# Attention outputs with features on the partitions, and probabilities scaled ahead of their transpose, in a six-layer transformer kernel

## The reference, cut to what matters

```python
for i in range(4):                       # first block: kinds A, B, C, A
    h = (mixer_a, mixer_b, mixer_c)[i % 3](x, ...)
    x = layer_norm(ALPHA * x + h, ...)
    x = layer_norm(ALPHA * x + swiglu(x, ...), ...)
# second block, twice: four branches (convolution, sparse attention over the
# 64 best keys, a gated recurrence, attention over 256 memory rows), gated,
# projected and added; then a gated feed-forward
```

## Time and profile before

| | |
|---|---|
| median of 3 runs | 2409.44 us (2409.36 to 2410.32) |
| span of the profiled execution | 2408.6 us |
| PE busy | 2375.2 us (99%) |
| PEld busy | 2001.8 us (83%) |
| DVE busy | 1633.0 us (68%) |
| ACT busy | 1122.9 us (47%) |
| POOL busy | 184.1 us (8%) |
| PE's share of the chain that ended last | 92% |

### The profile page before, as it was taken

The page is one execution under the profiler, slowest core; times in us unless marked ns, Lnnn a source line. Parts: engine busy times, 40 slices in busy tenths (PEclk is TensorE's granted clock), DMA queues, the critical chain, the costliest instruction groups (busy, mean ns, idle before and its releaser), DMA issues.

```text
span 2408.6 us, 33578 instructions
## 1 busy us (share of the span) xinstructions
PE 2375.2 (99%) x13648; PEld 2001.8 (83%) x13648; DVE 1633.0 (68%) x2282; ACT 1122.9 (47%) x1570; POOL 184.1 (8%) x190
## 2 busy tenths in 40 slices
PE   7999999999999999999999999999999999999999
PEld 5788888787888878887888888888888888988887
DVE  7866755557667576668776777677676577687664
ACT  4544344444443434435443455564444365574442
POOL 1210002021000320001100100000000000001000
PEclk9999999999999999999999999999999999999999
DMA  6465343335553446543755344444755344445652
GB/s 247 142 202 209 140 175 140 141 140 171 197 209 140 163 165 215 191 158 128 262 188 179 136 175 157 155 179 149 279 180 188 113 167 156 173 175 181 225 177 91
DMA packets 259080, 419.09 MB, mean 174 GB/s; under 512 B 11984, under 2 KB 149200, under 8 KB 258928
## 3 DMA queue, kind: packets, MB, share of 16 engines
q1 hardware_dynamic: 254064, 400.15, 46.7%
q0 software_dynamic: 4864, 16.80, 2.1%
HBM read 415.86 MB, written 1.05 MB: 173 GB/s over the span
## 4 chain that ended last, share of the span: by engine, by line
PE 92%; DVE 4%; ACT 2%; DMA 1%; issue 1%; POOL 0%; SPq 0%; DVEq 0%; ACTq 0%
PE bank_L L2431 21%; PE bank_L L2447 17%; PE bank_S L2811 8%; PE bank_T L2776 7%; PE bank_L L2776 7%; PE bank_O L2811 7%; PE bank_L L2428 4%; PE bank_T L2781 4%; PE bank_L L2781 4%; PE bank_O L2724 1%; DVE wlo L1631 1%; PE bank_S L2431 1%; PE bank_O L2431 1%; PE bank_T L2398 1%; PE bank_T L2707 1%; PE bank_T L2386 1%
## 5 line engine op out<-in xcount | busy, mean ns | idle before, releaser
L1631 DVE TENSOR_TENSOR wlo<-raw,whi 128x2048 fp32r<-128x2048 f32 x316 | 718.0, 2290 | 123.4 <-ACT whi L1237 123.0
L1237 ACT ACTIVATE whi<-raw 128x2048 fp32r<-128x2048 f32 x290 | 542.5, 1894 | 55.3 <-DMA raw<-in_w_out 13.2
L2431 PE MATMUL bank_L<-whi,xt 128*128 128x512 f32 (+2 forms) x1632 | 495.8, 386 | 3.3 <-ACT tok L1283 2.1
L2447 PE MATMUL bank_L<-whi,xt 128*128 128x512 f32 x1248 | 389.2, 393 | 3.3 <-DVE xt L1645 2.1
L2431 PEld LDWEIGHTS bank_L<-whi,xt 128*128 128x128 f32 x1632 | 295.9, 188 | 61.2 <-ACT tok L1283 3.3
L2431 PE MATMUL bank_L<-wlo,xt 128*128 128x512 f32 (+2 forms) x816 | 311.4, 382 | 0.0
L2447 PEld LDWEIGHTS bank_L<-whi,xt 128*128 128x128 f32 x1248 | 230.6, 188 | 51.9 <-DVE arena L1737 2.9
L1503 ACT ACTIVATE tok<-tok 128x256 f32<-128x256 f32 x96 | 40.1, 417 | 449.5 <-DVE tok L2137 449.5
L2447 PE MATMUL bank_L<-wlo,xt 128*128 128x512 f32 x624 | 243.6, 390 | 0.0
L2776 PE MATMUL bank_T<-xt,whi 128*128 128x512 f32 x768 | 192.3, 392 | 0.0
L2776 PE MATMUL bank_L<-xt,whi 128*128 128x512 f32 x768 | 191.7, 392 | 0.0
(11 more groups left out here) (353 smaller groups left out, 3630.3 us busy)
## 6 DMA issues: line engine op xcount, KB each, us to landing
raw<-in_w_gate_up SPq DMA_DIRECT2D x176, 512.0 KB, 5.9
raw<-in_w_in SPq DMA_DIRECT2D x72, 1024.0 KB, 6.8
draw<-in_w_down SPq DMA_DIRECT2D x44, 1024.0 KB, 6.2
raw<-in_ffn_w_up SPq DMA_DIRECT2D x88, 512.0 KB, 5.8
raw<-in_b_w_qkv SPq DMA_DIRECT2D x36, 1024.0 KB, 6.9
draw<-in_ffn_w_down SPq DMA_DIRECT2D x22, 1024.0 KB, 6.2
raw<-in_w_lift SPq DMA_DIRECT2D x16, 1024.0 KB, 6.2
raw<-in_a_w_qkv SPq DMA_DIRECT2D x12, 1024.0 KB, 8.2
```

The lines of the kernel that those rows point to most:

```text
L1237: act.activation(wide(whi, w, nkc, ncols)[:, ks, :], wide(raw, w, nkc, ncols)[:, ks, :], ACT.Copy) \
L1631: dve.tensor_tensor(wide(wlo, w, nkc, ncols)[:, ks, :], wide(raw, w, nkc, ncols)[:, ks, :], wide(whi, w, nkc, ncols)[:, ks, :].bitcast(F32 ...
L2431: mm = pe.matmul(banks[name][:, 0:st["ncols"]], xx[:, kk, t * P:(t + 1) * P], ww[:, kk, :], start=(kk == 0 and q == 0), stop=(kk == nkc - ...
L2447: mm = pe.matmul(banks[bank][:, :], xx[:, k, t * P:(t + 1) * P], ww[:, k, :], start=(k == 0 and q == 0), stop=(k == KC - 1 and q == 2))
```

## The change

It does the following things at once.

1. The product with values is turned round: the values (128 keys by 64 features) are the weights, and the transposed probabilities are streamed, 128 or 256 columns at a time. The even head of a pair writes partitions 0 to 63 of bank_O and the odd one 64 to 127. The output is there with features on the partitions, as the projection reads it. One bank holds four heads over 256 queries, and is held until it is split.
2. The transposes of the output (`turn_group` for these attentions, L2491), the evacuation to `r` or `arena`, and the later `halves`/`split` stages are gone. ACT copies bank_O into the high part (`group_high`), DVE subtracts for the low part (`group_low`), once for each bank. In B and C half of it goes to `yt_hi`, `yt_lo`, and half to `xt_hi`, `xt_lo`.
3. A query's sum is no longer on the partitions at the end, so the probabilities are scaled before their transpose. PE now waits for `scaled` where it waited for `p_done`.
4. In A and the sparse attention a new stage kind, `spread`, takes the place of `attention`. POOL scales (two instructions for a head, of 128 and 256 columns). The transpose comes three steps after the scores in A (two before), and still two in the sparse attention, where the products with values come up to one step later and for two heads at once. `sm` is a ring of five heads in A and of four in the sparse one, `pts` a ring of four.
5. In B and C ACT scales, in the same step as the exponentials. DVE takes the reciprocals of step i in step i (before: those of step i-1), ahead of `group_low`, rotations and `wlo` subtractions.
6. The rotations' scratch moves from `hg_values` to `r`.

The core of the diff:

```diff
 # POOL, kind "spread"
+                        pool.wait_ge(rl_done, k + 1)
+                        for row, (c0, c1) in enumerate(((0, P), (P, 3 * P))):
+                            q = slice(u["ps"] + c0, u["ps"] + c1)
+                            ins = pool.tensor_scalar(smflat[:, q], smflat[:, q], rl[:, k % 4, row:row + 1], None, ALU.mult)
+                        ins.then_inc(scaled, 1)
 # ACT, kind "paired"
-                    def pair_evacuate(j):
+                    def pair_scales(j):
                         act.wait_ge(rl_done, U0 + j + 1)
-                        act.wait_ge(pv_done, U0 + j + 1)
...
+                                ins = act.activation(smflat[:, q], smflat[:, q], ACT.Copy, scale=rl2[:, c:c + 1])
+                            ins.then_inc(scaled, 1)
+                    def group_high(g):
+                        to = st["to"]
+                        act.wait_ge(pv_done, V0 + (g + 1) * to["per"])
...
                         if 1 <= i <= len(J):
                             pair_copies(i - 1)
-                        if i >= 2:
-                            pair_evacuate(i - 2)
+                        if i < len(J):
+                            pair_scales(i)
+                        if i >= 2 and (i - 1) % st["to"]["per"] == 0:
+                            group_high((i - 2) // st["to"]["per"])
 # DVE, kind "paired"
+                    def group_low(g):
+                        to = st["to"]
+                        hi, lo = to["dst"][g]
+                        dve.wait_ge(thi_done, to["sg"] + g + 1)
+                        dve.tensor_tensor(lo, banks[st["ob"][g % 2]][:, :].rearrange("p (k s) -> p k s", s=SEQ), hi.bitcast(F32),
+                                          ALU.subtract).then_inc(tlo_done, 1)
...
                             pair_copies(i - 1)
-                            pair_reciprocal(i - 1)
+                        if i < len(J):
+                            pair_reciprocal(i)
+                        if i >= 2 and (i - 1) % st["to"]["per"] == 0:
+                            group_low((i - 2) // st["to"]["per"])
                         if i in st["ropes"]:
                             rotated(st["ropes"][i])
 # PE, kind "paired"
-                            pe.wait_ge(p_done, u["p0"] + 1)
+                            pe.wait_ge(scaled, u["sc0"] + 1)
...
+                        for two in zip(*(u["pv"] for u in J[j])):
+                            for w, (c, width, v, o1, first, last) in enumerate(two):
+                                c += J[j][w]["pts"]
+                                mm = pe.matmul(banks[name][w * HD:(w + 1) * HD, o0 + o1:o0 + o1 + width], v, pflat[:, c:c + width],
+                                               start=first, stop=last)
 # PE and DVE, kind "spread"
+                        pe.wait_ge(scaled, at["sc"] + i + 1)
...
+                    for i in range(st["steps"]):
+                        if i < len(U):
+                            maxima(i)
+                        if 1 <= i <= len(U):
+                            reciprocal(i - 1)
+                        if i > lag + 1 and (i - lag - 1) % 4 == 0:
+                            group_low((i - lag - 1) // 4 - 1)
+                        if 0 <= i - lag < len(U):
+                            copies(i - lag)
+                        if i in st["lows"]:
+                            split_lo(*st["lows"][i])
+                    group_low(len(U) // 4 - 1)
```

More of the change, by code:

```diff
@@ L498, in paired, with spread @@
                     n["tp"] += T
-                for g, when in at_groups.get(j, ()):
-                    turned["at_tp"][g], turned["when"][g] = n["tp"], (o_done, st["at"]["unit"] + when)
-                    n["tp"] += 1
             n["unit"] += len(pairs)
-            if turned:
-                for g in range(4):
-                    if turned["at_tp"][g] is None:
-                        turned["at_tp"][g], turned["when"][g] = n["tp"], (o_done, n["unit"])
-                        n["tp"] += 1
-            return st
+            n["pv"] += len(pairs)
+            return st
+        def spread(units, ready, first, behind, to, lag, ring, stride, lead=2, fill=(), lows=None, highs=None):
+            add("spread", units=units, ready=ready, first=first, behind=behind, to=to, lag=lag, lead=lead, fill=fill,
+                qb=SB if fill else QB, lows=lows or {}, highs=highs or {}, steps=len(units) + lag + 1)
+            for st in behind:
+                st["deferred"] = True
+            for st in fill:
+                st["kind"] = "fill"
+            for i, u in enumerate(units):
+                edge, ps = 1 if u["sink"] else 0, stride * (i % ring)
+                u["ps"], u["pts"] = ps + edge, 3 * P * (i % 4)
+                u["ends"] = ps
+                u["exp"] = [slice(ps, ps + edge + P), slice(ps + edge + P, ps + 3 * P + 2 * edge)]
+            n["seg"] += len(units)
+            n["ttr"] += T * len(units)
+            for q in ("p", "sc", "tp", "pt", "unit"):
+                n[q] += len(units)
+            n["pv"] += len(units) // 2
+            return (pv_done, n["pv"])
         def ffn(lhs, w_up, w_dn, alpha, evacuate=False, mem=None):
@@ L651, in build @@
                         dst = vv[g] if which == 2 else next_tok()
-                        after = [(o_done, n["unit"])] if which == 2 and n["unit"] else []
+                        after = [(pv_done, n["pv"])] if which == 2 and n["unit"] else []
                         if (which, g) == (2, 2):
@@ L1464, in _ @@
                             copies(i - 2)
-                        if st["rows"] and i == steps - 1:
-                            group_hi(st["rows"], 0)
-                            group_hi(st["rows"], 1)
                         if i >= 3:
@@ L2110, in _ @@
                             split_lo(*st["splits"][i])
-                        for g, _ in st["groups"].get(i, ()):
-                            group_lo(st["rows"], g)
                 elif st["kind"] == "ffn":
```

311 lines of the change are left out of this document (201 added, 110 removed).

## The result

The changed kernel takes 2439.31 us (median of 4 runs, 2435.62 to 2443.13) where the kernel before took 2409.4. The ratio is 1.0127, 95% interval 1.0113 to 1.0142: about 30 us slower. The prediction was 2409.7 with a range of 2400 to 2420, so the sign and the size are both missed. The span of the profiled execution is 2440.7 us, 32.1 more than before. It is the slowest of the four: its mean granted clock is 0.992, that of the other three 0.994.

A forecast was written before the change was run, and what follows sets the result against it. PE was taken to bound the kernel (busy 2375.2 of 2408.6 us), with DVE becoming A's bound. A -2.0, sparse -3.8, B +3.85 and C +2.2 sum to +.25, so 2409.7 us, range 2400 to 2420.

The forecast's parts named there:

- POOL's price: A: POOL's two scalings of a head take .95 us, between about .75 and 1.1, hidden under DVE's 1.27.
- DVE becomes the bound and the loop stays as long as it was: A: DVE needs 2.84 us per two heads, PE's old time; only the end gains, -1.0 a layer.
- The value products: Value blocks of two heads: .80 for 1.00 in A; in B 1.55 to 1.4, counted as -.7.
- halves of the array don't pair up: Rival: even and odd heads' streams into partition halves cost more than the narrow form; 2439 us, chance .04.
- the last rival: The change doesn't do what it says: removed instructions are covered by as many others; 2409 us, chance .04.
- three waits for bank_L: B: ACT's scalings delay bank_L's evacuation in three steps, by +.75, +1.0 and +1.25, together +3.0 us.
- dear scaling: Rival: ACT's scaling costs what the exponential does, .94, adding +4.5 in B and C; 2414.2 us, chance .12.
- The rotation at the end of the half: B, end of first half: bank copy and subtraction come before the rotation, so PE's transpose is +2.45 us later.
- +2.55 at the rotation: C, step 3: reciprocal, scalings, bank copy and subtraction now precede the rotation, making PE's transposes 2.55 us later.
- the sparse attention in sign and place: Two sparse layers: PE is gap-free, so removed work counts; -1.9 us each, after +.35 for head 0's wait.
- the cover that was missing: B and C: queues leave no slack at late places; the rival, that cover holds (2402 halfway), had chance .25.
- The rival of POOL and DVE blocking each other: A: DVE's two-column copies wait about .3 us for POOL's instructions, +9.6 over 32 heads; 2419.3 us, chance .13.

The follow-up runs named there:

- e1: Changed kernel with POOL's two scalings of a head in A cut to 8 columns each, result not normalised there: 2436.77 us, 29.0 over before.
- e12: Changed kernel with A's transposes four steps behind the scores instead of three: 2436.07 us, 29.2 over the kernel before.
- e9: Changed kernel with A's PE transposes moved ahead of the scores and DVE's copies ahead of the maxima: 2445.82 us, 38.4 over before.
- e13: Changed kernel with A's transposes four steps behind scores and another ACT and DVE order in B and C: 2416.54 us, 9.6 over before.
- e8: Kernel before the change, with the multiplications of C's step 3 rotation done five times: 2416.94 us, 9.1 over before.
- e3: Changed kernel with all work kept but another order on ACT and DVE in B and C: 2417.56 us, 9.8 over the kernel before.
- e7: Kernel before the change, with the multiplications of C's step 3 rotation done twice: 2411.22 us, 3.4 over before.

## Why the prediction was wrong

**POOL's price (A).** The step "for 128 and 256 columns: about .75 by the first, about 1.1 by the second" had both ends too low. The slope of 2 ns a column came from 8 and 16 columns, where 16 ns lie between two durations that are almost all start; the measured one is (927 - 607) / 128 = 2.5 ns, and the start .29, not .18. With 1.53 for a head POOL is above DVE's 1.27, and the sentence "so either is hidden but for the last head" fails: PE waited 4.3 us for scaled heads in the first A. But the price is not what A lost, since with the scalings cut to 8 columns (e1) as much was lost in other waits.

**"DVE becomes the bound and the loop stays as long as it was" (A).** This step failed: no wait of PE in the loop stood in the sum, and PE waited 7.0 us, for scaled heads and for copies. It compared rates. My account is that the loop is a chain: a head's way from scores to transposable probabilities (scores .86, maxima .86, exponentials .9, reciprocal behind the next maxima, POOL 1.53) against three steps, and values that wait for a copy behind the maxima. This is argued, not shown. e1 fits it (the waits stay with POOL's work taken away), but one step more (e12) gave some 0.8 us for both A together, of a rest of 5.3, and e9 made it worse. What is shown is that neither POOL's work nor ACT's help sets the time, and, by e13's trace, that with four steps DVE is the slowest engine, slowed by POOL. I had looked at each engine's sum and at the end of the loop, not at the way through it.

**The value products.** These were right. -.2 for two heads was taken in A, -.7 in B. From the start of a block to the start of the next, the four products of two heads cost .80 in A and in the sparse attention where 1.00 stood, as forecast. In B's first half:

```profile
439.80 1.53 PE L2742 MATMUL bank_O<-pts,arena 128*64 128x128 f32 x24
441.26 0.87 PE L2721 MATMUL bank_T<-ident,sm 128*128 128x128 f32 x6
```

1.46 against 1.55 before, and the narrow blocks .81 against .85: about half of the gain that was hoped for (1.4 and .75). This also settles the rival "halves of the array don't pair up". Its number, 2439, is the measured one by luck: its mechanism did not happen. Nor did that of the last rival: PE has 880 instructions fewer and ACT 96 (DVE has 2282 in both, where the prediction had its count fall).

**B.** PE at the places that the sum spoke of, and at the one that it didn't:

```profile
430.80 0.73 PE L2546 MATMUL bank_L<-whi,xt 128*128 128x512 f32 x2 [1.73 <-ACT tok L1323]
...
457.72 1.54 PE L2513 MATMUL bank_T<-ident,tok 128*128 128x128 f32 x6 [2.75 <-DVE tok L1820]
...
552.57 0.58 PE L2546 MATMUL bank_L<-whi,xt 128*128 128x256 f32 x2 [2.01 <-ACT arena L1323]
...
568.40 0.88 PE L2742 MATMUL bank_O<-pts,arena 128*64 128x128 f32 x12 [3.43 <-DVE xt L2201]
```

The three waits for bank_L were forecast at +.75, +1.0, +1.25 and are +1.04, +1.24, +1.54 (1.73, 1.93, 2.01 against .69, .69, .47): the mechanism was right, and the gap is the scaling's .93 in place of .75, the rival with "dear scaling". (That rival's own sum doesn't come out: six waits with two blocks each at .2 and C's four at .1 are 2.8, not 4.5.) The rotation at the end of the half was forecast at +2.45 and waits 2.75 against .32: +2.43. Missing from the sum were the waits for bank_O (3.43 and 1.2, the first for DVE's subtraction): a bank that holds four steps of one half is refilled only when it is split, and the split stands behind two scalings of .93. It was written in the change's description and not followed to PE.

**C.** +2.55 at the rotation, measured +3.87 (4.88 less 1.01). The queue is 2.9 of it: ACT was done with the exponentials at 861.94 - .24 = 861.70, and the rotation started at 864.56, the scalings being 1.50 where 1.1 was taken. The other part is POOL: its conversions now run beside two instructions of the rotation instead of one. In the kernel before, one already took 1.12 beside a conversion, where .28 is the time alone, which also means that 0.8 of the wait of 1.01 in the earlier trace rows was POOL's and not the queue's:

```profile
842.97 1.12 DVE L1753 TENSOR_TENSOR tok<-hg_values 128x128 f32<-128x128 f32 x1
```

**The clock.** No term at all. Each wait was costed once. By the windows PE ran at half the clock behind the long ones, and e8 measures 2.8 us for one such place. Of the 32 us, 17.5 are at the clock's account in the traced execution and the rest are the waits less the work removed. No rival has the clock either.

**Right:** the sparse attention in sign and place (-1.3 each instead of -1.9; PE waits 1.21 for head 0 where .35 was given, .58 of which is POOL's price), the value products, the places of the waits in B and C, and what moves them: the cover that was missing at the earlier trace rows was there once e3 had changed the queues. The rival of POOL and DVE blocking each other is real but small in the changed kernel: the copies of two columns have a mean of .195 where it was .150, 1.4 us for all 32. With POOL never idle (e13) the mean is .238, and in the loop's middle most take .36, as shown above (behind the count: shortest, median and longest ns):

```profile
L2082 DVE COPY sm<-sk x32: 148/192/380, 55.0 to 1144.2; 128x2 f32<-128x2 f32 x32
```

## What to carry to other kernels

When an operation is added to an engine with much idle time, write down what is queued behind it in each step and who waits for that: here the same work in another order was worth 20 us, more than leaving the work out. Look at the way of one item through a software pipeline as well as at each engine's sum, and test with a run what sets its pace: here both kinds of account missed. Before a trace's stretches are compared, take off what the clock took in each. A price from operations of 8 columns is no price for 256, and where PE is busy all the time, a wait of several us has to be counted with what the clock takes behind it.

## What the runs showed of the hardware

- Behind a wait of 7.3 us PE ran at 1.2 GHz for a while, at a cost of 2.8 us (e8); behind one of 2.8 us it did not in the traced execution (e7). Executions of one kernel differ in how often the clock falls, which spreads their times: e1 took 2431.79 us at a mean granted clock of 0.997 and 2435.96 to 2439.68 at 0.993 and 0.994.
- DVE's instructions with two operands in SBUF took 1.01 and 1.12 us beside a conversion on POOL, and 0.28 alone. The Trainium skill, "SBUF — State Buffer", section "Who interferes with whom", says that a VectorE instruction with two SBUF inputs contends with one of GpSimd that reads SBUF, for a pair of ports that is an exclusive lock; the trace agrees at 865.56: the two instructions end at 866.57 and 867.61, just behind POOL's two conversions, which end at 866.43 and 867.47. The prediction looked for this in A only, not where rotations meet conversions.
- DVE's copy of two columns took 0.15 us before the change and 0.36 in the middle of e13's A, beside scalings of 0.6 and 0.9 on POOL: it is held up, by less than the length of POOL's instruction.
- ACT's scaling of 768 columns (.93) costs as much as exponentials with their sum (.94), and POOL needs about twice ACT's time for the same scaling of 256 columns (.93 against .49).
- Twelve products of 128 columns into the two partition halves of a bank cost 1.46 us where twenty-four of 64 columns cost 1.55 (two heads in B), six .81 against .85 for twelve, and four of 128 and 256 columns .80 against 1.00 for twelve of 64 (A).
